# The first projections of a fused transformer kernel: queries summed while x arrives, x and memory turned in other places

## The reference, cut to what matters

```python
h = _rmsnorm(x, attn_norm_g[l])                       # x: 512 tokens x 1024 features
proj = jnp.einsum('bsd,dc->bsc', h, w_in[l])          # 1024 x 3080
fq, fk, fv, sq, sk, sv, f_logit = jnp.split(proj, split_at, axis=-1)
log_f = jax.nn.log_sigmoid(f_logit + b_forget[l])     # 8 heads
fox_o = _fox_attention(heads(fq), heads(fk), heads(fv), log_f)
...
m = _rmsnorm(mem, mem_norm_g[l])                      # memory: 256 tokens x 1024 features
x = x + _memory_cross_attention(h, m, w_mq[l], w_mkv[l], w_mo[l])
```

## Time and profile before

| what | value |
|---|---|
| median of 3 runs | 2068.57 us (2066.1 to 2068.95) |
| the profiled execution, its own time | 2069.1 us |
| its span in the profile | 2065.8 us |
| PE busy | 2014.6 us, 98% |
| DVE busy | 1155.7 us, 56% |
| ACT busy | 757.4 us, 37% |
| POOL busy | 203.9 us, 10% |
| DMA | 180.5 MB, 87 GB/s over the span |
| mean granted clock of PE | 0.993 |

### The profile page before, as it was taken

One profiled execution on the slowest core, in us unless ns is written; L12 is line 12 of the kernel. 1 busy time (PEld: TensorE's weight loads), 2 busy tenths in 40 slices (PEclk: granted clock), 3 DMA queues, 4 the chain that ended last, 5 costly groups with the idle time before them and its releaser, 6 DMA issues. The chain is left out here.

```text
span 2065.8 us, 23160 instructions
## 1 busy us (share of the span) xinstructions
PE 2014.6 (98%) x9535; PEld 1668.3 (81%) x9535; DVE 1155.7 (56%) x1585; ACT 757.4 (37%) x1201; POOL 203.9 (10%) x108
## 2 busy tenths in 40 slices
PE   7999999999999999999999999999999999999998
PEld 5897888788888888788878888888877788888887
DVE  6543576568756666846557643543487665333333
ACT  4354354235433333533223422233343443322224
POOL 1000000000000000000000222222221002122221
PEclk9999999999999999999999999999999999999999
DMA  5231212212233233233312233223223012232321
GB/s 167 83 99 45 82 62 72 92 42 86 98 102 100 85 102 102 82 106 98 102 62 82 88 102 102 85 99 102 82 66 102 21 62 84 100 102 91 95 101 61
DMA packets 141224, 180.51 MB, mean 87 GB/s; under 512 B 9664, under 2 KB 102976, under 8 KB 141120
## 3 DMA queue, kind: packets, MB, share of 16 engines
q1 hardware_dynamic: 139232, 177.52, 26.5%
q10 hardware_dynamic: 1632, 1.51, 0.2%
q0 software_dynamic: 256, 0.02, 0.0%
HBM read 176.91 MB, written 2.10 MB: 87 GB/s over the span
## 5 line engine op out<-in xcount | busy, mean ns | idle before, releaser
L432 PE MATMUL bank<-h_hi,w_hi 128*128 128x512 f32 x1376 | 542.4, 394 | 7.1 <-DVE arena L1556 4.5
L433 PE MATMUL bank<-h_lo,w_hi 128*128 128x512 f32 x1376 | 537.3, 391 | 0.0
L434 PE MATMUL bank<-h_hi,w_lo 128*128 128x512 f32 x1376 | 537.3, 390 | 0.0
L1649 ACT ACTIVATE w_hi<-raw 128x1024 fp32r<-128x1024 f32 (+2 forms) x336 | 332.7, 1033 | 512.4 <-PE bank L434 456.3
L432 PE MATMUL bank<-g_hi,w_hi 128*128 128x512 f32 (+1 forms) x988 | 384.1, 389 | 9.6 <-DVE g_lo L958 4.3
L434 PE MATMUL bank<-g_hi,w_lo 128*128 128x512 f32 (+1 forms) x988 | 378.8, 383 | 0.0
L433 PE MATMUL bank<-g_lo,w_hi 128*128 128x512 f32 (+1 forms) x988 | 378.7, 383 | 0.0
L402 POOL TENSOR_TENSOR w_lo<-raw,w_hi 128x1024 fp32r<-128x1024 f32 (+1 forms) x78 | 189.5, 2430 | 1658.9 <-ACT w_hi L1649 1658.9
L1002 DVE TENSOR_TENSOR resid<-bank,resid 128x512 f32<-128x512 f32 x288 | 195.9, 689 | 263.2 <-PE bank L434 262.8
L944 DVE TENSOR_TENSOR w_lo<-raw,w_hi 128x1024 fp32r<-128x1024 f32 (+1 forms) x258 | 304.8, 1206 | 67.7 <-ACT w_hi L1649 66.8
L432 PEld LDWEIGHTS bank<-h_hi,w_hi 128*128 128x128 f32 x1376 | 259.4, 189 | 64.5 <-issue 11.0
(11 more groups left out here) (199 smaller groups left out, 1686.8 us busy)
## 6 DMA issues: line engine op xcount, KB each, us to landing
raw<-w SPq DMA_DIRECT2D x64, 1024.0 KB, 5.2
raw<-w_up SPq DMA_DIRECT2D x22, 1024.0 KB, 5.1
raw<-a_w_in SPq DMA_DIRECT2D x16, 1024.0 KB, 5.2
raw<-w_in SPq DMA_DIRECT2D x12, 1024.0 KB, 5.4
raw<-w_down SPq DMA_DIRECT2D x11, 1024.0 KB, 4.9
raw<-w_mkv SPq DMA_DIRECT2D x8, 1024.0 KB, 5.5
raw<-a_w_out SPq DMA_DIRECT2D x8, 1024.0 KB, 5.0
raw<-w_out SPq DMA_DIRECT2D x4, 1024.0 KB, 5.0
```

Source lines behind the costliest of these rows:

```text
L432: nc.tensor.matmul(dst, a_hi, b_hi, start=(k == 0), stop=False)
L433: nc.tensor.matmul(dst, a_hi, b_lo, start=False, stop=False)
L434: last = nc.tensor.matmul(dst, a_lo, b_hi, start=False, stop=(k == n - 1))
L1649: A(hi, src, ACT.Copy).then_inc(w_hi_done, 1)
```

## The change

Line numbers in the text are those of the kernel before, except in the rows of the change's own order below.

- **Query weights as row chunks.** Chunk 0 is now rows 0 to 511 of w_in for all 512 query columns, chunk 1 rows 512 to 1023. Chunk 0 is loaded in two halves with a semaphore each.
- **Four tiles together.** PE sums all four query tiles at once, feature tile by feature tile: for k = 0 to 3, the 12 passes of k for four banks, then one tile of x is turned (`turn_x(k + 2)`); then tiles 6 and 7 are turned; then query tile after query tile k = 4 to 7.
- **x in other banks.** x is turned into `x_bank` (the banks of the attentions and statistics), with semaphores `x_full` and `x_copied`. DVE's copy of tile n stands ahead of the low half of tile n - 1, as before; its `split_low` pieces now lie among them, and so do ACT's `split_high` pieces.
- **x on two queues.** Pieces 1 and 3 of x are issued by ACT, behind the vectors; SP issues half of chunk 0, piece 0, the other half, piece 2, chunk 1, the memory.
- **Forget logits** go straight behind the queries, into `f_bank`, and DVE takes them after the queries.
- **Memory turned between keys.** After each of the four key tiles PE turns two tiles of the memory. DVE and ACT copy and split them there. The memory's statistic moves in between the halves of the values.
- ACT loads its first function table with a small copy, before the first weights are there.

```diff
-    out = [("tiles", KT)] + w_in(0) + [("tiles", KT), columns("w_in", 6 * HEADS * HD, n=HEADS, tiles=1)]
-    out += w_in(1) + tokens("w_in", 2) + mkv(0, 1, 2, 3) + tokens("w_in", 5) + w_in(3) + w_in(4)
+    out = tokens("w_in", 0) + [columns("w_in", 6 * HEADS * HD, n=HEADS, tiles=1)]
+    out += [columns("w_in", HEADS * HD, tiles=3), columns("w_in", HEADS * HD + COLS, tiles=6), ("tiles", 2)]
+    out += tokens("w_in", 2) + mkv(0, 1, 2, 3) + tokens("w_in", 5) + w_in(3) + w_in(4)
...
+        x_bank = [s_bank[1], pt_bank, o_bank, s_bank[0]]
...
# SP
-                if c == 1:
-                    for q in range(4):
+                if c == 0:
+                    v = w["w_in"].rearrange("(k p) n -> p k n", p=P)
+                    for j in range(2):
+                        sp.dma_start(quarter_view(raw, 0)[:, 2 * j:2 * j + 2, :], v[:, 2 * j:2 * j + 2, 0:512])\
+                          .then_inc(w_first[j], 16)
+                        q = 2 * j
                         sp.dma_start(x_stage[:, :, 256 * q:256 * q + 256], x_cols[:, :, 256 * q:256 * q + 256])\
                           .then_inc(x_loaded[q], 16)
...
# PE
+            def first_part(n, k):
+                if n == 0 and k % 2 == 0:
+                    pe.wait_ge(w_split, k // 2 + 1)
+                if n == 0:
+                    pe.wait_ge(h_ready, k + 1)
+                cut = slice(P * n, P * n + P)
+                stationary = [tuple(quarter_view(v, q // 4)[:, q % 4, cut] for v in (w_hi, w_lo)) for q in range(KT)]
+                return split_sum(tile_bank[n][:], stationary, h_tiles(), part=range(k, k + 1))
+            turn_x(0)
+            turn_x(1)
+            for k in range(4):
+                for n in range(4):
+                    first_part(n, k)
+                turn_x(k + 2)
+            turn_x(6)
+            turn_x(7)
+            for n in range(4):
+                for k in range(4, KT):
+                    last = first_part(n, k)
+                full(last)
+                if n == 2:
+                    stat(sq_x[:, 0, :], by_col=True)
...
+            for n in range(4):
+                by_feature(first=n % 2, tiles=n % 2 + 1, pair=True)
+                turn_mem(2 * n)
+                turn_mem(2 * n + 1)
+            by_token(between=lambda: stat(sq_mem[:, 0, :], NMEM, by_col=True))
...
# DVE
+            def take_x(n):
+                dve.wait_ge(x_full, n + 1)
+                V.tensor_copy(x[:, n, :], x_bank[n % 4][:]).then_inc(x_copied, 1)
+            split_low(1)
+            take_x(0)
+            lo_h(0, "attn_norm_g")
+            split_low(1)
+            for n in range(1, KT):
+                take_x(n)
+                if n >= 2:
                     lo_h(n - 1, "attn_norm_g")
+                if n in (5, 7):
+                    split_low(1)
...
# ACT
+            for q in (1, 3):
+                act.dma_start(x_stage[:, :, 256 * q:256 * q + 256], ...)
```

More of the change, by code:

```diff
@@ L446, in w_tiles, with by_feature @@
                 return [(view(w_hi, slot)[:, k, cut], view(w_lo, slot)[:, k, cut]) for k in range(n)]
-            def by_feature(tiles=2, moving=None, arrive=None, n_tokens=S):
+            def by_feature(tiles=2, moving=None, arrive=None, n_tokens=S, first=0, pair=False):
                 wait_chunk()
-                for j in range(tiles):
+                for j in range(first, tiles):
                     dst = next_bank()[:, 0:n_tokens]
@@ L454, in by_feature @@
                                    arrive if j == 0 else None))
-                chunk.n += 1
+                if tiles == 2 or not pair:
+                    chunk.n += 1
             def token_part(first, half, t, ks, arrive=None):
@@ L605, in _, with turn_x, turn_mem @@
             last.then_inc(vec_t, 1)
-            turn(x_stage, TT, S, x_loaded)
+            def turn_x(n):
+                if n % 2 == 0:
+                    pe.wait_ge(x_loaded[n // 2], 16)
+                if n == 3:
+                    pe.wait_ge(own, 1)
+                if n >= 4:
+                    pe.wait_ge(x_copied, n - 3)
+                for t in range(TT):
+                    last = nc.tensor.transpose(x_bank[n % 4][:, P * t:P * t + P], x_stage[:, t, P * n:P * n + P], ident[:])
+                last.then_inc(x_full, 1)
+            def turn_mem(n):
+                if n == 0:
+                    pe.wait_ge(mem_loaded, 16)
+                b = next_bank()
+                for t in range(MT):
+                    last = nc.tensor.transpose(b[:, P * t:P * t + P], mem_stage[:, t, P * n:P * n + P], ident[:])
+                full(last)
             def mem_keys(piece):
@@ L1099, in mem_values_of, with head_queries @@
                 take(two_tokens)
-            def head_queries(rows, each_chunk=lambda: None):
+            def head_queries(rows, then):
                 for n in range(4):
@@ L1121, in fox_keys @@
                     take(two_heads)
[L1122 to L1123 removed]
+                    then(n)
             def sb_keys(each_chunk):
@@ L1759, in _ @@
             split_high()
-            split_high()
             tile.n += 4
-            for n in range(KT):
-                taken()
-                high_half(m_hi[:, n, :], mem_t[:, n, :], gain("mem_norm_g", n))
-                squares(sq_mem, n, mem_t[:, n, :])
-            split_high()
-            tile.n += 1
             made.n += 1
@@ L1775, in _ @@
             acts.n += 1
-            tile.n += 4 + 4
-            split_high()
+            for n in range(4):
+                if n != 2:
+                    split_high()
+                tile.n += 1
+                for k in (2 * n, 2 * n + 1):
+                    taken()
+                    high_half(m_hi[:, k, :], mem_t[:, k, :], gain("mem_norm_g", k))
+                    squares(sq_mem, k, mem_t[:, k, :])
+            tile.n += 4
             root(rstd[:, 1, 0:NMEM], rstd_col[:, 4:6], stat_bank[:, 0:NMEM], col_bank[:, 0:2], D)
-            split_high()
             split_high()
```

106 lines of the change are left out of this document (55 added, 51 removed).

## The result

The changed kernel takes 2076.03 us (median of 5 executions, 2073.59 to 2079.22), the kernel before 2067.56 us in the same measurement (5 executions, 2066.10 to 2068.95): a ratio of 1.0043, with an interval of 1.0031 to 1.0055. It is slower by 8.5 us. 2074.8 was predicted, with a range of 2069.5 to 2080. The profiled execution is the fastest of the five, 2073.59 us with a span of 2071.4; it lies 4.5 above the profiled execution of before (2069.1), and its span 5.6 above that one's (2065.8).

A forecast was written before the change was run, and what follows sets the result against it. PE, busy 98% of the span, was taken as the bound; the terms up to the attention's start sum to +6.2 us on the profiled 2069.1, giving 2075.3, less 0.5 to the median: 2074.8 us, range 2069.5 to 2080.

The forecast's parts named there:

- first pass: Head: the first pass needs only x tile 0 and starts at 12.2 instead of 17.51, -5.3 us (-6.7 to -4.7).
- three x steps: Before k = 1, 2, 3: PE waits for DVE's low half behind the next copy, 2.1 us each, +6.3 (5.4 to 6.9).
- behind k = 3: At k = 4, 5, 6: PE waits for x tiles and weight pieces on DVE, +5.8 us (4.5 to 6.5).
- first key chunk: Before the key passes: its low half stands on DVE behind two query tiles, +1.5 us (0.5 to 2.5).
- memory: Turning between key tiles: 3.6 us with two bank waits of 0.9, instead of 5.9; -2.3 (-4.1 to -1).
- clock: behind the memory: The half-clock stretch after the memory's turn goes away, -1.5 us.
- clock: first passes: The slow clock at the first passes stays, so even; ends -1.7 and +0.5 us.
- clock: behind k = 3: One slow-clock stretch falls from the end of k = 3 to k = 6, +1.7 us (0 to +3.4).
- the second term: The waits at k = 4, 5, 6 for x tiles and weight pieces on DVE, +5.8 us.
- The rival on the faster side: Head: x steps overlap, PE runs nearly without gaps from 12.2; sum -7.1, some 2061.5 us; 6%.
- The landing of x: Head: piece 0 of x lands at 8.7 us again (7.3 to 9.3), since two queues share the DMA engines.
- the third rival: Slower still: clock falls in the x steps too or twice behind, 2077 to 2079; wholly half rate +7 more; 12%.

The follow-up runs named there:

- e2: The changed kernel with DVE making the low half of x tile n ahead of the copy of tile n + 1, n = 1 to 4: 2067.74 us (1.0002).
- e3: The changed kernel with PE turning x tile k + 2 in the middle of the twelve passes of k, DVE's order kept: 2068.69 us (1.0003).
- e4: The changed kernel with both weight pieces of chunk 1 split ahead of the copy of x tile 5: 2071.14 us (1.0017).
- e8: The changed kernel with all four x pieces issued by SP: 2077.23 us, or 2075.72 without one execution of 7222.04 (1.0036 without it).
- e9: The changed kernel with e2's order, earlier weight pieces, x on SP alone, earlier x statistic, ACT's second-key-chunk high half ahead of the forget functions: 2063.14 us (0.9979).
- e1: The changed kernel measured once more, with no edit: 2076.16 us, ratio 1.0042 against the kernel before.
- e7: The changed kernel with DVE splitting the first key chunk ahead of the first query tile instead of behind the second: 2074.14 us (1.0035).
- e5: The kernel before with only the memory turned between the key tiles; x, queries and forget logits as before: 2064.57 us (0.9982).
- e10: e5 with ACT's function table also loaded ahead of the first weights: 2060.82 us, ratio 0.9969 against the kernel before.

## Why the prediction was right, and where it was off

The sum was made to the attention's start. Here each term is taken from the profile of the change, from start to start of PE's rows, less the time of the passes between. What a pass takes more behind a wait (restarts) is a row of its own.

| term | predicted | in the profile |
|---|---|---|
| first pass | -5.3 | -5.8 (17.51 to 11.67) |
| three x steps | +6.3 | +6.2 (2.05, 2.14, 2.04) |
| behind k = 3 | +5.8 | +5.2 (3.17, 0.45, 1.60) |
| first key chunk | +1.5 | +1.5 (54.90 to 56.59, less a pass) |
| memory | -2.3 | -2.6 (0.35, 1.41, 1.19, 0.36 for 5.9) |
| clock: behind the memory | -1.5 | -1.5 |
| clock: first passes | 0 | +0.6 (twelve in 5.02, nine in 3.72 before) |
| clock: behind k = 3 | +1.7 | 0 here, +2.0 where it falls |
| restarts | not counted | +1.1 (estimate, below) |
| sum | +6.2 | +4.7, of 4.85 measured |

**Right.** The mechanism, place by place: the three waits at k = 1, 2, 3 of about 1.5, for `h_lo`; three thin places behind k = 3; the wait at the first key chunk for DVE's `w_lo`. e2 and e3 show it from two sides, e4 for the second term. The rival on the faster side was the order of PE alone, "turned two tiles ahead"; its steps without a gap came only when DVE's order or the place of the transposes was changed as well.

**How near the number is.** The measured median is 1.2 us from the forecast, but that is in part luck. The forecast added 6.2 us to a median of before of 2068.57; in the measurement that median was 2067.56, and the difference 8.5. The sum's own object, the attention's start, moved by 4.85. That is less than 6.2 because the slow stretch of 1.7 didn't come and four terms were a few tenths too high (3.2 in all with it), while the restarts and the slower passes of k = 0 (1.7) weren't counted. What the medians have beyond the profiled pair the prediction did not foresee, and it stays open.

**The landing of x.** 8.7 was taken, between 7.3 and 9.3. It was 8.08 in the change (7.82 to 8.18 in the six other runs with two queues), and 7.07 and 7.35 in series (e8, e9). So the sharing gave back part of the 1.5 us, not all of it.

**The memory.** Two waits of 0.9 for banks were foreseen. There were two, at the right turns (69.09 above, and one at 75.85), of 0.60 and 0.39. The 12.4 against 11.6 us of that step was too coarse for a difference of under a microsecond, and the parts that are named for the 12.4 (2.8, 1.2, 4.6, 2.0, 1.2) add up to 11.8, which would have left a wait of 0.2. The bank came 12.5 us after the first key pass (56.59 to 69.09), so the chain had been named rightly and 12.4 was near, and the sum of the term came out.

**Restarts.** A pass that follows a wait or a group of transposes takes 0.31 to 0.34 us until the next, instead of 0.23 (18.74 to 19.07, for one). Around a dozen of these, at 0.1 us each, make some 1.1 us by this estimate. The sum had no term for it.

**The clock.** This is the term whose size was right and whose occurrence was not known. The stretch behind k = 3 kept the full clock in the profiled executions of the change and of e1, and lost it in those of e7 and e8, with the same waits there. When it falls it lasts 6.8 us, not the 3.7 of the first passes of before, but PE waits for DVE in a part of it, so it costs 2.0. The median of the change lies 2.4 above its profiled execution. But that of before lies 1.5 to 2.1 above its fastest one in each measurement, and behind the attention's start the profiled executions of e7 and e8 took 1970.6 and 1969.9 us against 1966.4, with slow stretches in places that the change doesn't touch (the row at 200.10 above is one). So how much of the 8.5 us between the medians belongs to the stretch behind k = 3 these runs don't settle. The medians of e2, e3 and e4 lie below e1's by 2.2 to 2.5 us more than their attention starts earlier. That would fit a loss in the change's usual executions that its two profiled ones don't have, but it is one median, e1's, that all three are compared with.

**The x steps.** They did not run at half rate, as the third rival had it: the granted clock was full from 16.69 to 31.43, with PE at work in 10.32 of 14.74 us. By the rule that the prediction took from the Trainium skill (TensorE: Matmul & The Clock Gate, "The HAM clock gate": slow by default, released by activity) they might have; the trace doesn't bear that out here.

The twelve passes of k = 0, behind a head with transposes alone, were slow: the first took 0.57 us to the next, nine 0.43 each, the last two 0.38 and 0.23. The first nine of before had taken 0.41 each. In before the profile grants half the clock there. In the change its column shows the full clock from the start of the span, so here it is the pace that tells, not the column.

## What to carry to other kernels

Work that is prepared ahead on one engine is only ahead if the engine that finishes it has it in that order too: look, at each hand-over, for an instruction that waits for something newer in front of the one that the bound engine wants. In an in-order queue the half that is wanted next goes ahead of the copy for the step after, or the producer is moved up into the middle of the cover. And take a change with several parts apart: here one part gained 3.3 us by itself, and one of the small ones, loading the function table while the weights are under way, another 1.2 on the first pass, while the largest lost it all, and even with its orders put right has shown no gain over the old one (e9 against e5 and e10).

## What had not been expected

- An idle bracket undercounts a gap. The three waits sum to 4.4 us, and removing them gave 5.2, start to start.
- DVE, busy 56% over the span, is nearly full behind k = 3: 7.54 of 8.17 us. In the x steps before it is busy for 4.05 of 14.74 us and is late all the same, by its order alone.
- A wait in front of another can be its cover. e7 took away the one for the first key chunk, and PE waited as much longer for a bank, whose chain runs over ACT's functions and which DVE's order ahead of them doesn't shorten.
- Two profiled executions with the same waits behind k = 3 had the full clock, two had half of it for 6.8 us. Nothing in the rows ahead of them tells which it will be.
- The landing of the first piece of x moved by 0.5 to 1.0 us when a piece that nobody wants yet was taken off the other queue, with the same bytes ahead of it on its own.
